# Split weights of the projection stages kept in DRAM and reloaded; mixed rows and residual fetched back before the stage barrier

## What is computed

```
m = concat(attn, rwkv) @ w_out                 # token mixing, then the output projection
x = x + rms_norm(m)
c = softmax(q k^T / sqrt(128)) v @ w_mem_o     # q = rms_norm(x) @ w_mem_q, 4 heads, 256 memory rows
x = x + rms_norm(c)
f = (silu(h @ w_gate) * (h @ w_up)) @ w_down   # h = rms_norm(x)
x = x + rms_norm(f)
```

## Time and profile before

| what | value |
|---|---|
| runs | 4364.46, 4365.15, 4369.7 us; median 4365.15 us |
| profiled execution | 4369.05 us; span on the core 4367.5 us, mean granted TensorE clock 0.903 |
| TensorE matmuls | 3600.6 us busy, 82% of the span |
| VectorE, ScalarE, GpSimd | 1902.8, 1477.8, 98.9 us |
| DMA | 241.49 MB, mean 55 GB/s |

### The profile page before, as it was taken

One profiled execution on the slowest core, in us unless ns is written; L12 is line 12 of the kernel. 1 busy time (PEld: TensorE's weight loads), 2 busy tenths in 40 slices (PEclk: granted clock), 3 DMA queues, 4 the chain that ended last, 5 costly groups with the idle time before them and its releaser, 6 DMA issues. The chain is left out here.

```text
span 4367.5 us, 86654 instructions
## 1 busy us (share of the span) xinstructions
PE 3600.6 (82%) x32908; PEld 3329.3 (76%) x32908; DVE 1902.8 (44%) x2817; ACT 1477.8 (34%) x2683; POOL 98.9 (2%) x134
## 2 busy tenths in 40 slices
PE   4888689967675999999649886998578679999994
PEld 3878557757665999999648784777477579999994
DVE  3345355624655333333452453565356543333334
ACT  3334354425564111111242433453355531111113
POOL 0000000000000000000000100000000000000000
PEclk9999779968887999999879996899689789999997
DMA  4111210004210111111121212000332101111111
GB/s 167 48 59 59 72 34 24 9 25 164 74 63 29 41 51 43 48 43 43 39 98 41 69 59 63 19 28 10 121 92 82 45 21 52 43 48 43 43 48 49
DMA packets 282804, 241.49 MB, mean 55 GB/s; under 512 B 26452, under 2 KB 260388, under 8 KB 281728
## 3 DMA queue, kind: packets, MB, share of 16 engines
q1 hardware_dynamic: 273600, 193.23, 14.5%
q0 software_dynamic: 8896, 44.07, 2.7%
HBM read 198.63 MB, written 38.63 MB: 54 GB/s over the span
## 5 line engine op out<-in xcount | busy, mean ns | idle before, releaser
L692 PE MATMUL PS<-HH,WH 128*128 128x352 f32 (+3 forms) x3712 | 1248.3, 336 | 171.0 <-PEq L676 171.0
L692 PE MATMUL PS<-HH,WL 128*128 128x352 f32 (+3 forms) x3712 | 1218.5, 328 | 0.0
L692 PE MATMUL PS<-HL,WH 128*128 128x352 f32 (+3 forms) x3712 | 1215.3, 327 | 0.0
L692 PEld LDWEIGHTS PS<-HH,WH 128*128 128x128 f32 x3712 | 725.8, 196 | 194.1 <-issue 189.7
L692 PEld LDWEIGHTS PS<-HH,WL 128*128 128x128 f32 x3712 | 725.6, 195 | 3.1 <-issue 1.2
L692 PEld LDWEIGHTS PS<-HL,WH 128*128 128x128 f32 x3712 | 722.6, 195 | 0.0
L2158 DVE TENSOR_TENSOR WL<-WRAW,WH 128x1024 fp32r<-128x1024 f32 x194 | 241.2, 1243 | 656.9 <-DVEq L2157 656.9
L1389 ACT CAST WH<-WRAW 128x1024 fp32r<-128x1024 f32 x258 | 270.3, 1048 | 666.4 <-ACTq L1394 604.2
L1357 PE MATMUL PS<-GH,WH 128*128 128x352 f32 x1056 | 339.6, 322 | 0.0
L1357 PE MATMUL PS<-GH,WL 128*128 128x352 f32 x1056 | 339.6, 322 | 0.0
L1357 PE MATMUL PS<-GL,WH 128*128 128x352 f32 x1056 | 339.6, 322 | 0.0
(11 more groups left out here) (303 smaller groups left out, 4918.2 us busy)
## 6 DMA issues: line engine op xcount, KB each, us to landing
WRAW<-in_w_gate_up SPq DMA_DIRECT2D x88, 512.0 KB, 3.7
WRAW<-in_w_out SPq DMA_DIRECT2D x48, 512.0 KB, 4.0
WRAW<-in_w_down SPq DMA_DIRECT2D x46, 512.0 KB, 3.5
WRAW<-in_w_in SPq DMA_DIRECT2D x38, 512.0 KB, 3.7
raw_dram<-MIX SPq DMA_DIRECT2D x24, 528.0 KB, 3.5
R<-raw_dram SPq DMA_DIRECT2D x24, 512.0 KB, 3.5
WRAW<-in_w_mem_q SPq DMA_DIRECT2D x24, 512.0 KB, 3.6
WRAW<-in_w_mem_o SPq DMA_DIRECT2D x24, 512.0 KB, 3.3
```

Of the source, the lines that this page charges most:

```text
L692: ins = e.matmul(out, lhs(k, wp), rhs(k, xp), start=first, stop=(k == n - 1 and xp == 1))
```

## The change

Two things are done, in both layers.

First, each weight tile of OUT, QUERY and BACK is split only for the first token part. Once DVE has made the low half, POOL stores both halves (512 KB each) to the new `split_dram`; for the second and third part SP loads both halves back into the tile's slot, without ACT and DVE. `split_here(i)` says which tiles are still split: 0 to 7, 24 to 27, 36 to 39, and 48 and up.

Second, what stood between mixing and OUT is moved ahead. The last prompt pair and the sample tokens write their mixed rows straight into R2; SP no longer stores them. The sample's masked scores move out of R2 into a row set of pair 2 that is no longer used (`LTS`). POOL loads mixed rows 0 to 3 and seven rows of the residual once the last pair's rows are prepared, and mixed rows 4 to 6 once the last pair's masks are used; the shift rows are made during the sample pair (`shift_out`) and stored there. Behind the barrier remains the eighth residual row.

```diff
+    split_dram = nc.dram_tensor("split_dram", [P, 16, 2, 1024], F32, kind="Internal").ap()
...
+    LTS = rows_of(PAIRS - 2, BB)[:, 0:1024].rearrange("p (a t) -> p a t", a=4)
...
+    def split_here(i):
+        return i >= STAGE_TILES or any(0 <= i - first < count for first, count in zip(FIRST_TILE, (8, 4, 4)))
+
+    def kept_as(i):
+        kind = max(k for k in (OUT, QUERY, BACK) if FIRST_TILE[k] <= i)
+        return (0, 8, 12)[kind] + (i - FIRST_TILE[kind]) % (8, 4, 4)[kind]
...
@@ SP
+                if j == PAIRS - 1:
+                    break
                 e.wait_ge(S("y_ready"), 1)
...
+            give(e, "rows_saved")
...
-            e.dma_start(mix_dram[:, 4:8, SEQ:T], rows_of(PAIRS, RR).rearrange("p (j t) -> p j t", j=PAIRS)[:, :, 0:DEC_SEQ]).then_inc(S("mix_stored"), 16)
-            stored()
             give(e, "mix_saved")
...
+            def split_back(*tiles):
+
+                for i in tiles:
+                    e.wait_ge(S("slot_free"), 1)
+                    e.sem_inc(S("slot_free"), -1)
+                    if split_here(i - TILE_SLOTS):
+                        e.wait_ge(S("stored_sp"), 1)
+                        e.sem_inc(S("stored_sp"), -1)
+                    for half, dst in enumerate((wh_of(i), wl_of(i))):
+                        e.dma_start(dst.bitcast(F32), split_dram[:, kept_as(i), half, :]).then_inc(S(f"back_full{i % TILE_SLOTS}"), 16)
...
+            for n in range(4, DB):
+                w8(n % 2, io["w_out"], l, n * P)
+            split_back(*range(8, 11))
+            query_weights(0, 1)
+            split_back(*range(11, 24))
+            query_weights(2, 3)
+            back_weights(0, 1)
+            split_back(*range(28, 36))
+            back_weights(2, 3)
+            gate_up_weights(0)
+            split_back(*range(40, 48))
...
@@ POOL
+            e.wait_ge(S("rows_over"), 1)
...
+            move(R2[:, 0:4, :], mix_dram[:, 0:4, :])
+            move(R1[:, 0:7, :], x_spill[:, 0:7, :])
+            e.wait_ge(S("masked_over"), 1)
...
+            e.wait_ge(S("rows_saved"), 1)
...
+            move(R2[:, 4:7, 0:SEQ], mix_dram[:, 4:7, 0:SEQ])
             e.wait_ge(S("shc_ready"), 1)
...
-            moved(4)
+            moved(7)
             e.wait_ge(S("mix_saved"), 1)
             e.sem_inc(S("mix_saved"), -1)
             barrier(e, "pool")
-            for b in range(DB):
-                e.dma_start(R2[:, b, :], mix_dram[:, b, :]).then_inc(S(f"mix_in{b}"), 16)
-            move(R1[:, :, :], x_spill)
...
+            def split_out(*tiles):
+                for i in tiles:
+                    if i >= 2:
+                        e.wait_ge(S("split_done"), 1)
+                        e.sem_inc(S("split_done"), -1)
+                    for half, src in enumerate((wh_of(i), wl_of(i))):
+                        move(split_dram[:, kept_as(i), half, :], src.bitcast(F32))
+                    moved(2)
+                    give(e, "stored_act" if split_here(i + TILE_SLOTS) else "stored_sp")
+
+            split_out(0)
+            move(R1[:, 7, :], x_spill[:, 7, :])
             moved()
             give(e, "x_back")
+            split_out(1)
...
             mem_in(0, "new_mem_k_prompt", "new_mem_v_prompt")
+            split_out(*range(2, 8))
+            split_out(*range(24, 28))
             e.wait_ge(S("ckr_free"), 1)
             e.sem_inc(S("ckr_free"), -1)
             mem_in(1, "cache_mem_k", "cache_mem_v")
+            split_out(*range(36, 40))
@@ PE
+            def shift_out():
...
+                take(7)
+                for g in range(2):
+                    ins = e.matmul(PS[g * 64:g * 64 + 16, 7 * 512:7 * 512 + P], SHC[:, g * 16:(g + 1) * 16], ident, start=True, stop=True)
...
                     last_state(last)
+                    if j == PAIRS:
+                        shift_out()
                     centred(last)
...
@@ ACT
             def split_tile(i):
-                if i < STAGE_TILES + 2:
+                if not split_here(i):
+                    give(e, "slot_free")
+                elif i < STAGE_TILES + 2:
+                    if i >= TILE_SLOTS and split_here(i - TILE_SLOTS):
+                        e.wait_ge(S("stored_act"), 1)
+                        e.sem_inc(S("stored_act"), -1)
                     e.wait_ge(S(f"w_full{i % 2}"), 16)
...
             for half in range(2):
-                e.wait_ge(S("mix_act"), 4)
-                e.sem_inc(S("mix_act"), -4)
                 copy(HH[:, 4 * half:4 * half + 4, part_span(0)], R2[:, 4 * half:4 * half + 4, part_span(0)]).then_inc(S("hh_ready"), 1)
@@ DVE
             def lo_tile(i):
-                if i < STAGE_TILES + 2:
+                if split_here(i) and i < STAGE_TILES + 2:
```

More of the change, by code:

```diff
@@ L498, in _, with query_weights, back_weights, gate_up_weights @@
+            def query_weights(*blocks):
+                for n in blocks:
                     w8(n % 2, io["w_mem_q"], l, n * P)
-            for c in range(3):
-                for n in range(4):
+            def back_weights(*blocks):
+                for n in blocks:
                     weight(n % 2, w_block(io["w_mem_o"], l, n * 2 * P, 2 * P, 4), view=lambda d: d.rearrange("p (k n) -> p k n", k=4))
-            with e.Fori(0, FB // 2) as i:
+            def gate_up_weights(n):
+                w8(0, io["w_gate_up"], l, n * P)
+                w8(1, io["w_gate_up"], l, n * P + D_FF)
@@ L644, in _ @@
             barrier(e, "pool")
-            for b in range(DB):
-                e.dma_start(R2[:, b, :], mix_dram[:, b, :]).then_inc(S(f"mix_in{b}"), 16)
-            move(R1[:, :, :], x_spill)
-            e.reg_add(mix_due, mix_due, 16)
-            mixed = e.snap(mix_due, min_val=16)
-            for b in range(DB):
-                e.wait_ge(S(f"mix_in{b}"), mixed)
-                give(e, "mix_act")
+            def split_out(*tiles):
[9 more added lines that the diff above has]
+            move(R1[:, 7, :], x_spill[:, 7, :])
             moved()
             give(e, "x_back")
+            split_out(1)
             def mem_in(g, ksrc, vsrc):
@@ L956, in level_left @@
                         at = a * 512 + g * CHUNK
[L957 removed]
+                        ins = e.matmul(PS[r, at:at + CHUNK], masked_part(j, 0, u)[r, g, :], XX[u][r, g, :], start=True, stop=True)
                     ins.then_inc(S("chain_for_scalar"), 1)
@@ L1197, in _ @@
                 give(e, f"bank{b}")
-            e.wait_ge(S("shc_full"), 1)
-            e.sem_inc(S("shc_full"), -1)
-            claim(0)
-            for g in range(2):
-                ins = e.matmul(PS[g * 64:g * 64 + 16, 0:P], SHC[:, g * 16:(g + 1) * 16], ident, start=True, stop=True)
-            ins.then_inc(S("shc_psum"), 1)
             barrier(e, "pe")
@@ L1698, in state_out, with shift_out @@
                 give(e, "bank6", "state_out")
+            def shift_out():
+                from_psum("shc_psum")
+                for g in range(2):
+                    ins = copy(AUX[g * 64:g * 64 + 16, 256:384], PS[g * 64:g * 64 + 16, 7 * 512:7 * 512 + P])
+                settled(ins)
+                give(e, "bank7", "shc_ready")
             def outputs(j, u):
@@ L1797, in sample_rows @@
                 if j == PAIRS - 1:
-                    give(e, "sam_ready", "sam_dve")
+                    give(e, "sam_ready", "sam_dve", "shc_full")
             def pair(j):
@@ L1857, in _ @@
             variances(PAIRS)
-            e.wait_ge(S("y_saved"), 2)
-            e.sem_inc(S("y_saved"), -2)
-            give(e, "shc_full")
-            e.wait_ge(S("shc_psum"), 1)
-            e.sem_inc(S("shc_psum"), -1)
-            for g in range(2):
-                ins = copy(AUX[g * 64:g * 64 + 16, 256:384], PS[g * 64:g * 64 + 16, 0:P])
-            ins.then_inc(S("act_done"), 1)
-            e.wait_ge(S("act_done"), 1)
-            e.sem_inc(S("act_done"), -1)
-            give(e, "bank0", "shc_ready")
+            e.wait_ge(S("y_saved"), 1)
+            e.sem_inc(S("y_saved"), -1)
             barrier(e, "act")
@@ L2590, in prepare @@
                     give(e, "set_ready", "set_act")
+                    if j == PAIRS - 1:
+                        give(e, "rows_over")
             def key_sums(j, *groups):
@@ L2660, in lo_tile @@
                     give(e, f"w_ready{i % TILE_SLOTS}", f"w_free{i % 2}")
+                    if i < STAGE_TILES:
+                        give(e, "split_done")
             def part(kind, c, n):
```

63 lines of the change are left out of this document (39 added, 24 removed).

## The result

The changed kernel takes **4316.74 us** (median of four runs, 4311.0 to 4321.47) against 4367.42 us (4364.46 to 4371.13) for the kernel before: ratio 0.9877, 95% interval 0.9857 to 0.9897. That is 51 us faster where 66 was forecast; 4316.74 lies inside the range and inside the likeliest case's own range. The profiled execution took 4318.23 us.

What follows compares the result with a forecast made beforehand. TensorE (PE), busy 82%, plus its waits and slow-clock stretches bound the kernel. Gains of 16.6 + 28.7 less 12.4 lost made 32.9 us a layer, 66 in two: 4299 us, range 4268 to 4338 (8 in 10).

Steps and rivals of the forecast that it cites:

- likeliest case's own range: Whole kernel: 4280 to 4318 us, from 6 to 7.5 us per tile store and a fifth of 28.7 either way; chance 0.52.
- Boundary: Between mixing and OUT: earlier loads let PE start at 978.4 instead of 994.69; 16.6 us gained a layer.
- Subtractions and casts that go: OUT, QUERY and BACK: 32 of 48 tiles lose a DVE subtraction and an ACT cast; 28.7 us gained a layer.
- PE hides the others: OUT to BACK: removed subtractions and casts not ahead of a late DVE signal gain nothing.
- The store chain: First part of OUT: POOL stores tiles one at a time, delaying PE's tile 10; 12.4 us lost a layer.
- constant C: First part of OUT: POOL's cycle for storing one tile's two halves, taken as 6.5 us, range 4.3 to 8.3.
- Mixing, 0 us: Mixing: the loads moved ahead into it were given no cost, 0 us.
- the 917 and 961 us marks: Mixing: prompt state store issued at 917.16, sample state at 960.60, both ahead of 971, so earlier loads are covered.
- Stores keep up: First part of OUT: tile stores take up to 5 us and cost nothing; 91 us gained, 4274 us; chance 0.20.
- Slow stores: First part of OUT: tile stores take 8.3 us; 37 us gained in all, 4328 us; chance 0.16.
- Rows late: Before OUT: POOL is held by a wait ahead of the barrier; 33 us less gain, 4332 us; chance 0.05.
- Pitch: Stores to `split_dram`: rows 128 KiB apart land slowly; at 13 us a tile 38 us slower, 4403 us; chance 0.07.

## Why the prediction was right, and where not

- **Boundary, 16.6 us: right.** 17.7 and 18.3 us. DVE's last mixed row ends at 980.06 and PE starts at 986.14, 6.1 us later, where 7 to 8 were expected and 23.7 stood before. POOL issues its first store at 980.90, 0.84 us behind that row: the barrier's estimate of 0.9. The 0.6 us for PE's shift product do not show: DVE's row ends 10.3 us behind the sample's state store, 10.4 before.
- **Subtractions and casts that go, 28.7 us: low, 36.1 measured.** DVE's cycle in the second part of OUT is 4.6 us, as forecast. OUT's first stretch gained 10.5 us without the stores (79.47 to 68.94) where 7.4 and 2.0 for the clock were taken; part 3 8.9 for 7.4; QUERY 4.2 for 4.3; BACK 6.3 for 7.6. "PE hides the others" failed: the cross-attention rounds gained 6.2 us, 5.4 of them idle time of PE (9.5 to 4.1 us of it). Most of QUERY's moved tiles fall among them: DVE and ACT issue 7 and 8 instructions less there and work 11 and 7 us less.
- **The store chain, 12.4 us: the mechanism right, the size low.** It cost 18.0 us in layer 0 and 16.8 in layer 1; what follows is layer 0. The forecast's sum ends with tile 10 there 67.4 us after the barrier (10.4 + 52 + 5.0); measured from POOL's first store it starts after 68.6 (980.90 to 1049.48). That closeness is partly luck, since the terms were off both ways: the eight stores took 49.7 us, not 52; the residual row and the keys 13.0, not 10.4 (their own sum, 4.3 + 5.9, is 10.2); the reload 5.9, not 5.0. The largest miss is the moment at which PE wants tile 10: without the stores it starts 46.7 us after OUT does, and OUT 5.2 after the barrier, so 52 and not 55. Together this makes 16.6 us, and 1.4 more come behind tile 10. The stops before tiles 4 and 8 and the slow clock behind them are parts of this lateness, not additions to it, since POOL's chain runs without a gap from 980.90 to 1043.56 and sets tile 10 whatever PE does before. A constant C was wrong: 5.0 to 5.3 us for tiles 2 to 5, but 10.0 and 8.3 for tiles 6 and 7, because the forecast did not see the reloads of tiles 8 and 9 beside them.
- The Trainium skill's page (DMA: Bandwidth & Descriptors, Anatomy of one DMA) gave an estimated 4.9 us for the pair. The trace agrees within some tenths for tiles 0 and 2 to 5 and not for the stores beside a reload, and the consequence, that the chain would then cost nothing, did not follow.
- **Mixing, 0 us: wrong, and the largest miss.** "Every load but the last residual row is issued earlier" was costed at nothing, with the 917 and 961 us marks as cover. Cover was there for POOL's waits, but not for the DMA engines that PE's instruction packets use: 9.2 and 10.0 us a layer by the marks (435.4 and 434.1 us less 426.7 and 424.1, and half a microsecond of later start in layer 0), of which 6 to 7 go with the burst. The forecast asked who waits behind the moved step on its queue, and not who shares the engines.
- **The sum.** Without mixing the layer gained 35.7 us, 2.8 more than forecast; mixing took 9.2 back. Layer 1 is much the same (24.3 us of the span's 50.8), and the total is 51 us. That it lies in the likeliest case's own range is in part luck: boundary and subtractions gave 8.5 us a layer more than forecast, which covered over half of the 14.8 that the chain and mixing took beyond it.
- **The rivals.** Stores keep up: no; four of the eight stores came near it, the mean of 6.2 did not, and the chain cost more than forecast. Slow stores: no. Rows late: no. Pitch: no, tested.

## What to carry to other kernels

A bulk load that is moved to an idle queue is not free because the queue is idle: look at what else uses the DMA engines then, the instruction packets among it, and put the burst where PE is waiting anyway. A chain of store, wait, store is priced by its last consumer: list for each later tile which landing it hangs on, ask which transfers run beside each store, compare the end of the chain with the moment at which the consumer would start without it, and keep two stores in flight rather than reorder the chain.

## What the runs showed of the hardware

- 5.8 MB in two transfers stopped PE for 2.0 to 3.1 us at "issue" in every layer of every run that had the burst there, and in no layer without it; in layer 0 of the changed kernel two of PE's instruction packets landed 3 and 6 us later than in the kernel before. That the late packets cause the stop is read from their times and from the runs with and without the burst; no run separates it from other contention of the same burst.
- The same burst in the sample part, where PE is busy for 29 of 44 us and at a clock of 0.62 anyway, cost nothing that can be seen.
- Two 512 KB stores to DRAM from POOL, waited for, cycle in 5.0 to 5.3 us beside raw tile loads, and in 8.3 and 10.0 us beside a reload of two 512 KB halves, which then takes up to 10 us itself. A pitch of 128 or 136 KiB makes no difference.
